# Regrouping the projections inside a chunked recurrence, and starting the next product before the stage ends

## The reference, cut to what matters

```python
def rwkv7_step(state, inp):
    r, decay, k, v, kk, a = inp
    sa = jnp.einsum('bhij,bhj->bhi', state, -kk)
    state = (state * decay[:, :, None, :]
             + sa[..., None] * (kk * a)[:, :, None, :]
             + v[..., None] * k[:, :, None, :])
    out = jnp.einsum('bhij,bhj->bhi', state, r)
    return state, out

# hybrid_layer
    proj = x @ w_in
    pool_out = multiscale_pool(proj[..., :D_POOL], ...)
    rwkv_out = rwkv7_mix(proj[..., D_POOL:], ...)
    mixed = jnp.concatenate([pool_out, rwkv_out], axis=-1) @ w_out
    h = layer_norm_2(DEEPNORM_ALPHA * x + mixed, ln1_g, ln1_b)
    ffn = hierarchical_moe(h, router_group, ..., exp_down)
```

## Time and profile before

| | us |
|---|---|
| median of 3 runs | 3073.77 |
| lowest, highest | 3071.57, 3078.01 |
| the profiled execution, its own time | 3072.45 |
| its span (first to last instruction) | 3070.6 |
| PE busy in the span | 2856.3 (93%) |
| DVE, ACT, POOL busy | 1535.7, 724.2, 261.9 |

### The profile page before, as it was taken

The page is one execution under the profiler, slowest core; times in us unless marked ns, Lnnn a source line. Parts: engine busy times, 40 slices in busy tenths (PEclk is TensorE's granted clock), DMA queues, the critical chain, the costliest instruction groups (busy, mean ns, idle before and its releaser), DMA issues. The chain is left out here.

```text
span 3070.6 us, 52396 instructions
## 1 busy us (share of the span) xinstructions
PE 2856.3 (93%) x20752; PEld 1903.6 (62%) x20752; DVE 1535.7 (50%) x4101; ACT 724.2 (24%) x1655; POOL 261.9 (9%) x343
## 2 busy tenths in 40 slices
PE   3999989989999999999999999999999797999996
PEld 2787456664688545885445777777777554444442
DVE  4543056761455566655654566666666366011115
ACT  2211056551200000000003344343444200111111
POOL 0000011100000000000000222121222100101001
PEclk9999999999999999999999999999999897999998
DMA  5101023321023453224453000000000200999965
GB/s 202 47 28 55 0 98 103 110 78 41 28 83 110 153 176 123 93 106 154 169 187 132 17 11 25 3 25 25 2 25 3 101 35 21 347 350 357 350 249 192
DMA packets 103873, 338.88 MB, mean 110 GB/s; under 512 B 6864, under 2 KB 16592, under 8 KB 94560
## 3 DMA queue, kind: packets, MB, share of 16 engines
q1 hardware_dynamic: 95696, 306.35, 27.9%
q0 software_dynamic: 6912, 25.17, 2.2%
q10 hardware_dynamic: 1040, 4.19, 0.3%
HBM read 302.60 MB, written 33.10 MB: 109 GB/s over the span
## 5 line engine op out<-in xcount | busy, mean ns | idle before, releaser
L1840 PE MATMUL rwkv_ps<-all_main,pre_ws 128*128 128x256 f32 x1152 | 290.9, 389 | 0.0
L1183 PE MATMUL mlp_ps<-mlp_w2s,all_main 128*128 128x512 f32 x512 | 239.6, 592 | 0.0
L2761 PE MATMUL ex_pg<-all_main,ex_xT 128*128 128x512 f32 x512 | 225.5, 594 | 0.0
L1840 PEld LDWEIGHTS rwkv_ps<-all_main,pre_ws 128*128 128x128 f32 x1152 | 207.6, 190 | 28.9
L2207 DVE TENSOR_TENSOR all_tail<-rwkv_ps,all_tail 128x256 f32<-128x256 f32 x216 | 91.6, 424 | 191.4 <-PE rwkv_ps L1946 144.7
L1183 PE MATMUL mlp_ps<-all_main 128*128 128x512 f32 x384 | 183.2, 592 | 0.7 <-DVE all_main L1396 0.7
L2761 PEld LDWEIGHTS ex_pg<-all_main,ex_xT 128*128 128x128 f32 x512 | 97.6, 191 | 122.4 <-issue 122.4
L1183 PEld LDWEIGHTS mlp_ps<-mlp_w2s,all_main 128*128 128x128 f32 x512 | 96.6, 190 | 117.8 <-issue 105.4
L2151 POOL TENSOR_TENSOR all_tail<-all_tail,pre_cst 128x256 f32<-128x256 f32 x120 | 99.9, 847 | 472.9 <-DVE all_tail L2207 299.3
L2068 ACT COPY all_tail<-rwkv_ps 128x256 f32<-128x256 f32 (+1 forms) x216 | 83.0, 396 | 219.4 <-PE rwkv_ps L1937 184.2
L1183 PEld LDWEIGHTS mlp_ps<-all_main 128*128 128x128 f32 x384 | 72.7, 190 | 93.2 <-issue 69.4
(11 more groups left out here) (439 smaller groups left out, 5087.9 us busy)
## 6 DMA issues: line engine op xcount, KB each, us to landing
mlp_w2s<-in_w SPq DMA_DIRECT2D x64, 1024.0 KB, 4.9
all_main<-in_w_gu SPq DMA_DIRECT2D x32, 2048.0 KB, 9.8
all_early<-in_w SPq DMA_DIRECT2D x32, 1024.0 KB, 4.7
att_wa<-in_w_ada SPq DMA_DIRECT2D x32, 512.0 KB, 3.9
all_early<-in_w_d SPq DMA_DIRECT2D x16, 1024.0 KB, 11.7
all_main<-in_w_d SPq DMA_DIRECT2D x16, 1024.0 KB, 11.2
y_rows<-ex_y SPq DMA_DIRECT2D x32, 512.0 KB, 3.1
qkv_wq<-in_w_qkv SPq DMA_DIRECT2D x6, 2048.0 KB, 7.5
```

Of the source, the lines that this page charges most:

```text
L1183: last = nc.tensor.matmul(ps[:, PRODUCTS.index(name), :], lhsT=lhsT, rhs=rhs, start=j == 0, stop=j == FPAIRS - 1)
L1840: last = nc.tensor.matmul(ps[:, bank, 0:UT], lhsT=ws[:, n, k, :], rhs=xT[:, k, (col + NB) % S:(col + NB) % S + UT], start=(k == 0), stop=( ...
L2761: last = nc.tensor.matmul(pg[:, n % 2, :], lhsT=xT[:, n % 2, k, :], rhs=gu[n][:, k, :], start=(k == 0), stop=(k == KT - 1))
```

## The change

**One: the order of projections.** The sixteen k-tiles of r and v that stood in seven runs (2, 3, 3, 2, 2, 2 and 2 of them) stand in four runs of four: at l=0, and in levels 2, 3 and 5. Level 1, level 4 and the place behind level 5 have none. No instruction is added or taken away by it.

**Two: the mixing product's first tile.** `mix(0, ...)`, 16 matmuls, is taken out of `stage_mix_route` and becomes `mix_first(n)` in `stage_rwkv`: the first half of the columns ahead of pass 24's transposes, the second half behind them, in PSUM banks 0 and 1 of an allocation that both stages now share. Tile 0 needs the first 128 tokens of every pair of heads, and the last of these comes from unit 20, so its inputs are ready. `mix_first(0)` waits for unit 23's last copy by ScalarE (`y1`), for its last state (`st3`) and for unit 20's output; TensorE ends its block with a wait for all sixteen. The two LayerNorm rows are loaded inside the recurrence's block, once the gate's product of the last unit has read their place. In the mixing stage TensorE begins with tile 1 and waits for `c_in` only ahead of the first router product, and VectorE behind the first tile's normalisation.

```diff
                     def between(l):
 
                         if l == 0:
-                            project(0, range(0, 2), A_BANK)
-                        if l == 1:
-                            project(0, range(2, 5), A_BANK)
+                            project(0, range(0, 4), A_BANK)
...
-                            project(0, range(5, 8), A_BANK)
+                            project(0, range(4, 8), A_BANK)
                         if l == 3:
-                            project(2, range(0, 2), B_BANK)
+                            project(2, range(0, 4), B_BANK)
...
-                            project(2, range(2, 4), B_BANK)
                         if l == 5:
...
-                            project(2, range(4, 6), B_BANK)
+                            project(2, range(4, 8), B_BANK)
...
-                    project(2, range(6, 8), B_BANK)
...
+                def mix_first(n):
+                    if n == 0:
+                        pe.wait_ge(mix_in, 32)
+                        wait(pe, act_w, UNITS - 1, "y1")
+                        wait(pe, dve_w, UNITS - 1, "st3")
+                        wait(pe, dve_y, (PAIRS - 1) * WPAIRS, "y_out")
+                    for k in range(KT):
+                        nc.tensor.matmul(ps[:, n, :], lhsT=mixT[:, k, 0:P], rhs=main[:, k, D + n * NB:D + (n + 1) * NB],
+                                         start=(k == 0), stop=(k == KT - 1)).then_inc(mixed_first, 1)
+
                 pe.wait_ge(cleared, 2)
-                each_unit(pe, body)
+                each_unit(pe, body, mix_first)
+                pe.wait_ge(mixed_first, 2 * KT)
...
-                pe.wait_ge(c_in, 48)
-                for t in range(TT):
+                pe.sem_inc(mm, 1)
+                for t in range(1, TT):
...
+                    if t == 1:
+                        pe.wait_ge(c_in, 48)
+                    logits(t - 1)
```

More of the change, by code:

```diff
@@ L1690, in _, with stage_rwkv @@
                         dve.wait_ge(mapped, 2 * half + POOLED.index(n) + 1)
-def stage_rwkv(nc, main, tail, early, pre, w_rkv, lora_up, lora_in, w_mix, ident):
+def stage_rwkv(nc, ps, main, tail, early, pre, w_rkv, lora_up, ln_rows, lora_in, w_mix, ident):
     UT = 2 * P
@@ L1803, in each_unit @@
                 nxt = q + 1 < UNITS
+                if q == UNITS and around_last:
+                    around_last(0)
                 body(q, 0 if last else (q % WPAIRS + 1) * UT, (q + 1) // WPAIRS if last and nxt else None, q > 0, 0 <= q < UNITS, nxt)
+                if q == UNITS and around_last:
+                    around_last(1)
         with nc.Block() as block:
@@ L1819, in _ @@
                 sp.wait_ge(mix_in, 32)
+                sp.wait_ge(pe_a.sem, pe_a.at(UNITS - 1, "g"))
+                for n in range(2):
+                    sp.dma_start(lora_in[:, n, :], ln_rows[n].partition_broadcast(P)).then_inc(rows_in, 16)
+                sp.wait_ge(rows_in, 32)
             @block.tensor
@@ L2363, with stage_mix_route @@
 IOTA = GROUPS + EXPERTS + OVERFLOW + MAX_MORE
-def stage_mix_route(nc, mixT, ws, rows, ln_rows, hres, h_dram, w_router, b_router, counts_in, dest, wgt, over, tok_of_row, w_gu, w_d, gu, dn,
+def stage_mix_route(nc, ps, mixT, ws, rows, hres, h_dram, w_router, b_router, counts_in, dest, wgt, over, tok_of_row, w_gu, w_d, gu, dn,
                     ones, cumul, ident):
@@ L2418, in _ @@
             def _(sp):
-                for n in range(2):
-                    sp.dma_start(rows[:, n, :], ln_rows[n].partition_broadcast(P)).then_inc(r_in, 16)
                 sp.dma_start(wr[:], w_router).then_inc(c_in, 16)
@@ L3084, in second_program @@
     ident, ones, cumul = consts[:3]
[L3085 to L3097, removed]
+    with Scope(nc, "mixing") as x:
+        with Scope(nc, "pre") as p:
+            pre = Early(p, norm.rearrange("p t h -> p (t h)")[:, 0:PAIRS * WPAIRS * NPAR])
+            stage_pool(nc, main, tail, early, A["head_cols"], A["pool_w"], A["inv_count"], gates, gates[:, 1, :], xres, y_dram, ident, pre, A)
+            ps = x.ps("ps", [P, 8, NB])
+            stage_rwkv(nc, ps, main, tail, early, pre, A["w_rkv"], A["lora_up"], A["ln1"], gates, A["w_mix"], ident)
+        dest = scope.sb("dest", [P, 2, TT], I32)
+        wgt = scope.sb("wgt", [P, 2, TT])
+        over = scope.sb("over", [1, OVERFLOW + 1], I32)
+        tok_of_row = scope.sb("tok_of_row", [P, BLOCKS], I32)
+        own = early.rearrange("p (n f d) -> p n f d", n=2, f=2)
+        gu = [main[:, :, c:c + NB] for c in (2 * D, 2 * D + NB, D, D + NB)]
+        dn = [own[:, 0], own[:, 1], main[:, 0:2, 0:D], main[:, 2:4, 0:D]]
+        stage_mix_route(nc, ps, main[:, :, 0:D], main[:, :, D:2 * D], gates, xres, h_dram, A["w_router"], A["b_router"], A["counts"], dest, wgt,
+                        over, tok_of_row, A["w_gu"], A["w_d"], gu, dn, ones, cumul, ident)
     stage_experts(nc, h_dram, A["w_gu"], A["w_d"], gu, dn, main[:, 4:8, 0:D], over, tok_of_row, y_dram, ident)
```

16 lines of the change are left out of this document (6 added, 10 removed).

## The result

| | before | after |
|---|---|---|
| median, us (20 runs each) | 3074.93 | 3080.02 |
| lowest, highest | 3070.90, 3080.98 | 3075.37, 3086.56 |
| the profiled execution, its span | 3072.45, 3070.6 | 3079.54, 3077.7 |

The ratio is 1.0015 with the interval 1.0008 to 1.0022, that is 4.6 us more (2.5 to 6.8). A cost and a gain stand behind this small number, and both can be read off TensorE's own starts.

A forecast was written before the change was run, and what follows sets the result against it. TensorE's own list was taken to bound the recurrence, and TensorE's waits the seam behind it. +20.7 us for regrouped projections and -16.4 us for tile 0 gave +4.3 on 3072.45, so 3076.7 us, range 3070 to 3085.

The forecast's parts named there:

- Part one's size: Recurrence: regrouping projections adds 3.02 us and gives back 2.12, so 0.90 us per pass, 20.7 us over 23 passes.
- The step that took the emptied gaps from the unit without projections: Pass 23 shows empty gaps: level 1 at 1.15 us, level 4 at 1.15, behind level 5 at 1.21.
- Nothing late: Level 2's ScalarE copy keeps over 1 us of margin; VectorE's slack before the QT addition is used up almost exactly.
- The 2.3 us that I kept for it at the upper end: Allowance of 0.1 us per pass for VectorE's QT addition, counted only in the upper bound.
- rival of a late engine: VectorE or ScalarE late once a pass, at level 2's copy or QT addition: 9.2 us more, 3086 us; chance 0.10.
- The rival that had 24.6 us of waits of rows 2 shrink: Recurrence: early waiting is won back at TensorE's later recorded waits, leaving only the seam's gain, 3056 us; chance 0.10.
- Part two's size: Seam, last Y copy to tile 1: 31.26 us becomes 14.9, a gain of 16.4 us, bounds 14.5 to 16.9.
- The meeting of the stages: Engines meeting between recurrence and mixing stage, taken as 0.53 us, entered as 0.5 us in the seam's sum.
- instruction fetch: TensorE fetching instructions at the mixing stage's start could lose up to 1.9 us, making the seam's gain 14.5 us.
- the sum: Recurrence loss plus seam gain: +20.7 - 16.4 = +4.3 us, giving 3076.7 us; bounds +1.5 to +10.8 us.
- I would be wrong if the clock left 1.00 in the recurrence: Sign against the forecast: TensorE's granted clock falling in the recurrence; the falling-clock rival said 3115 us, chance 0.01.
- the argument from one trace: Last unit's levels ran at clock 1.00 with TensorE busy only 10.19 of 13.85 us, so emptied gaps leave it alone.

The follow-up runs named there:

- covered gaps: Kernel before with seven runs of 5, 1, 2 (r) and 3, 1, 3, 1 (v) k-tiles, no gap empty, tile 0 unmoved: 3075.92 us, ratio 1.0008.
- the repeated one: The changed kernel itself, unaltered, run again on the same chip as its parts: 3081.13 us, ratio 1.0024 against the kernel before.
- part one alone: Kernel before with only the seven projection runs made four runs of four, the mixing product left in its stage: 3095.89 us, ratio 1.0080.
- the empty level 1: Kernel before with only level 1's three k-tiles moved to l=0: 3081.42 us, run once.
- part two alone: Kernel before with tile 0's product in the recurrence, early loads and late wait, the old seven runs kept: 3060.45 us, ratio 0.9957.
- the three others: Kernel before with level 4 emptied (3078.07 us), with the place behind level 5 emptied (3086.67 us), or with early loads and late constants' wait only (3066.13 us).

## Why the prediction held

**Part one's size.** The step that took the emptied gaps from the unit without projections held to 0.01 us in all three places, and so did the 0.43 us of a moved projection. For a pass 0.90 us was predicted and 0.90 measured, for all 23 it was 20.7 and 20.8.

**Nothing late.** Level 2's copy by ScalarE ends at 2373.12 us, 1.23 us before t starts (1.07 before the change). VectorE's slack of 0.47 us ahead of the QT addition is used up, as reckoned: the addition now starts where the operation before it ends, with no idle time between. TensorE does not wait for it.

```profile
2387.99 0.42 DVE L2210 TENSOR_TENSOR all_early<-rwkv_rkv,all_early 128x256 f32<-128x256 f32 x1
2388.41 0.42 DVE L2222 TENSOR_TENSOR rwkv_QT<-mixing_ps,all_early 128x256 f32<-128x256 f32 x1
```

The 2.3 us that I kept for it at the upper end were not needed. The prediction's rival of a late engine was also drawn too tight: it let 0.05 us on VectorE decide. But the addition ends at 2388.83 us, 0.42 us before the first product that reads QT (L2010 at 2389.25), and before the change it was the same 0.42 (2367.18 and 2367.60). There was room left behind the addition, not only ahead of it.

**Waits regained: no.** The rival that had 24.6 us of waits of rows 2 shrink falls by the wait table above: they stayed. The reason given, that L2018 waits for a copy of L1968's own result, fits: its successor L2022 still waits 24 times, 10.9 us in all.

**Part two's size.** Predicted 14.9 us from the copy to tile 1, measured 15.07. The meeting of the stages was the term that was off: I took 0.5 us from VectorE's and GpSimd's meeting, while TensorE took 0.78 from the end of its last product (0.73 in two other traces), and 1.13 us where it came idle into the stage. This is the term that I had called instruction fetch and bounded by the 1.9 us of rows 9. The trace names the sequencer's branch and has no row for a fetch, so what fills the 0.78 us is not shown. Before the change it lay within the time that TensorE waited for the constants anyway.

**Missed.** The pass ahead of the first unit costs 0.4 us, which the sum left out: I counted 23 passes and took the one without levels as free, yet it has the same k-tiles and a wait of its own between them. The run with covered gaps bears this out from the other side: with six k-tiles of r ahead of that wait instead of five, the way from the recurrence's first matmul to the first L1883 is 21.37 us instead of 21.81. The prediction also said that I would be wrong if the clock left 1.00 in the recurrence. It did, for some 4 us in the last unit, and cost 0.9 us; see the last section. It was no consequence of the change, but the argument from one trace, that idle time of this size leaves the clock alone, does not hold for that unit. The sum was +4.3 us; the trace has +5.9 with both of these, the repeated one, at the full clock, +5.0, and the two ratios +4.6 and +7.4. That the first comparison came within 0.3 us of the sum is luck in the last microsecond; the terms are what was right.

## What to carry to other kernels

Work that fills the gap between two dependent products costs only what it adds to the wait that is there anyway. Here the first piece in a gap cost 0.09 us in level 1 and 0.03 behind level 5, 0.27 in level 4 where something else covered part of the wait, and every further one 0.43. So give each gap one piece before any gap gets a second. Beyond that it did not matter where they stood. The three runs that were joined away saved 0.19 us of TensorE's busy time for a pass, far less than the 0.33, 0.15 and 0.39 us net that the three emptied gaps lost; joining runs without emptying a gap was not tried. To know what an empty gap costs before trying it, look for a pass of the same loop that has nothing to put there, such as the last one. And at a stage's start look at what its first product really reads: the early wait for all of the stage's inputs was more than half of what this change won at the seam.

## What the hardware showed unasked

The granted clock fell to 0.50 (1.2 GHz) for some microseconds inside the last unit's levels in 4 of 10 traces. In the changed kernel it looks so (stretches of one microsecond, columns as above):

```profile
2430.00:2431.00 1.00, 0.75 (x16) 0.56 (x15) 0.00 (x0) 0.22 (x2) 0.17 (x1) 0.60 0.00 0
2431.00:2432.00 1.00, 0.79 (x14) 0.79 (x16) 0.00 (x0) 0.26 (x2) 0.56 (x1) 0.50 0.00 0
2432.00:2433.00 1.00, 1.00 (x26) 1.00 (x23) 0.42 (x1) 0.00 (x0) 0.00 (x0) 0.50 0.00 0
2433.00:2434.00 1.00, 0.92 (x20) 0.78 (x16) 0.67 (x3) 0.04 (x1) 0.00 (x0) 0.69 0.00 0
2434.00:2435.00 1.00, 0.62 (x20) 0.62 (x22) 0.00 (x0) 1.00 (x4) 0.72 (x1) 1.00 0.00 0
```

At half the clock the t product's row takes 1.12 us, its 0.68 us at the full one. Ahead of the fall TensorE had been idle 1.78 us before the product ahead of the levels, and 0.56 us before level 1's x. The unit is the same in all kernels, these idle times included, and the same stretch of the repeated run of the changed kernel reads 1.00:

```profile
2427.38:2441.22 13.84, 10.20 (x259) 8.66 (x259) 5.42 (x22) 3.94 (x12) 3.95 (x6) 1.00 0.01 4
```

The four are the changed kernel, part one alone, the covered gaps and the empty level 1. The kernel before, part two alone, the repeated run and the three others don't have it. So it isn't tied to the emptied gaps: the kernel with covered gaps has it, in its longest form (0.50 from 2404.5 to 2411.0 us, some 2.1 us lost), and there it comes straight behind the 1.78 us; two kernels with an emptied gap and the repeated run, with three, don't have it. The Trainium skill (TensorE: Matmul & The Clock Gate, "Why this matters for your kernels") has idleness drop the clock. As advice it does not say that gaps as short as the emptied ones do harm; that was the prediction's reading. The four traces agree with it, in the emptiest unit of the recurrence, and the other six, with the same idle times, show no fall. In the full passes, with up to 0.53 us of idle time in a gap, each of 74 stretches of 10 us of the changed kernel (1686 to 2426 us) reads 1.00. What decides between a trace with the fall and one without stays open.
